# Two transformer layers and a three-branch block on one core: the change from one stage to the next by column halves and quarters

## The reference

```python
h = x                                                    # (1, 256, 1024)
u = rms_norm(h, g_mix[0]);  h = h + mla_stick_breaking_mixer(u, ...)     # first mixer
u = rms_norm(h, g_ffn[0]);  h = h + swiglu(u, w_gate[0], w_up[0], w_down[0])
u = rms_norm(h, g_mix[1]);  h = h + chunk_band_mixer(u, w_qkv, rel_bias, w_out)   # band mixer
u = rms_norm(h, g_ffn[1]);  h = h + swiglu(u, w_gate[1], w_up[1], w_down[1])
h = rms_norm(h, g_final)
hn = rms_norm(h, ln_g_2)                                 # second block
proj = hn @ w_in_2
branches = (moba_attention, dilated_attention, swa_sink_attention) on parts of proj
out = h + (sum of sigmoid(gates) * (branch @ w_branch)) @ w_out_2

def swiglu(u, w_gate, w_up, w_down):
    return (jax.nn.silu(u @ w_gate) * (u @ w_up)) @ w_down
```

## Time and profile before

| | |
|---|---|
| median of three runs | 1051.57 us |
| the profiled execution | 1051.47 us, of which its span is 1049.5 us |
| PE busy | 998.5 us (95% of the span) |
| DVE, ACT busy | 633.9 us (60%), 593.0 us (57%) |
| POOL busy | 21.3 us (2%), 10.64 us of it the mask's addition |
| all DMA traffic | 170.23 MB, mean 162 GB/s |

### The profile page before, as it was taken

The page is one execution under the profiler, slowest core; times in us unless marked ns, Lnnn a source line. Parts: engine busy times, 40 slices in busy tenths (PEclk is TensorE's granted clock), DMA queues, the critical chain, the costliest instruction groups (busy, mean ns, idle before and its releaser), DMA issues.

```text
span 1049.5 us, 13511 instructions
## 1 busy us (share of the span) xinstructions
PE 998.5 (95%) x5026; PEld 816.8 (78%) x5026; DVE 633.9 (60%) x780; ACT 593.0 (57%) x912; POOL 21.3 (2%) x21
## 2 busy tenths in 40 slices
PE   4999789999998999989999998999999998999998
PEld 3888668888887777768888887788787886778876
DVE  3576567555555574665555555668567566766654
ACT  4677464544454564554544454666756575856561
POOL 1000004000000000010000000000000000000000
PEclk9999999999999999999999999999999999999999
DMA  7435156655655433368555655454343333335550
GB/s 232 146 117 200 41 200 193 207 188 173 200 162 198 161 123 121 118 212 291 197 190 171 200 163 197 145 177 161 126 154 120 120 121 121 121 121 200 176 185 40
DMA packets 105691, 170.23 MB, mean 162 GB/s; under 512 B 3843, under 2 KB 65210, under 8 KB 105652
## 3 DMA queue, kind: packets, MB, share of 16 engines
q1 hardware_dynamic: 103040, 161.23, 46.6%
q0 software_dynamic: 2288, 8.37, 2.3%
q10 hardware_dynamic: 324, 0.10, 0.0%
HBM read 168.58 MB, written 1.11 MB: 162 GB/s over the span
## 4 chain that ended last, share of the span: by engine, by line
PE 89%; ACT 5%; DVE 4%; issue 1%; DMA 0%; ACTq 0%; DVEq 0%
PE acc L442 14%; PE acc L402 13%; PE acc L404 12%; PE acc L403 12%; PE pair_ps L404 7%; PE pair_ps L402 7%; PE pair_ps L403 7%; PE acc L612 4%; PE turn_ps L524 2%; PE pair_ps L512 1%; PE acc L492 1%; PE pair_ps L511 1%; ACT w_hi L922 1%; PE turn_ps L460 1%; ACT logit L1045 1%
## 5 line engine op out<-in xcount | busy, mean ns | idle before, releaser
L1538 DVE TENSOR_TENSOR w_lo<-w_raw,w_hi 128x2048 fp32r<-128x2048 f32 (+3 forms) x156 | 351.2, 2256 | 154.6 <-ACT w_hi L922 154.2
L922 ACT ACTIVATE w_hi<-w_raw 128x2048 fp32r<-128x2048 f32 (+3 forms) x156 | 290.3, 1863 | 86.8 <-PE acc L404 47.4
L402 PE MATMUL acc<-w_hi,uT_hi 128*128 128x512 f32 (+3 forms) x552 | 221.3, 401 | 9.9 <-DVE w_lo L1538 6.0
L404 PE MATMUL acc<-w_hi,uT_lo 128*128 128x512 f32 (+3 forms) x552 | 213.8, 387 | 0.0
L403 PE MATMUL acc<-w_lo,uT_hi 128*128 128x512 f32 (+3 forms) x552 | 213.2, 386 | 0.0
L402 PEld LDWEIGHTS acc<-w_hi,uT_hi 128*128 128x128 f32 x552 | 105.2, 191 | 35.1 <-issue 8.9
L402 PE MATMUL pair_ps<-w_hi,uT_hi 128*128 128x512 f32 x320 | 126.6, 396 | 0.0
L404 PE MATMUL pair_ps<-w_hi,uT_lo 128*128 128x512 f32 x320 | 125.0, 391 | 0.0
L403 PE MATMUL pair_ps<-w_lo,uT_hi 128*128 128x512 f32 x320 | 124.7, 390 | 0.0
L404 PEld LDWEIGHTS acc<-w_hi,uT_lo 128*128 128x128 f32 x552 | 104.8, 190 | 21.4
L403 PEld LDWEIGHTS acc<-w_lo,uT_hi 128*128 128x128 f32 x552 | 105.3, 191 | 18.1
(11 more groups left out here) (210 smaller groups left out, 1269.0 us busy)
## 6 DMA issues: line engine op xcount, KB each, us to landing
w_raw<-in_w_in SPq DMA_DIRECT2D x46, 1024.0 KB
w_raw<-in_w_gate SPq DMA_DIRECT2D x44, 512.0 KB
w_raw<-in_w_up SPq DMA_DIRECT2D x44, 512.0 KB
w_raw<-in_w_down SPq DMA_DIRECT2D x22, 1024.0 KB
w_raw<-in_w_out SPq DMA_DIRECT2D x12, 1024.0 KB
w_raw<-in_w_qkv SPq DMA_DIRECT2D x16, 512.0 KB
w_raw<-in_w_branch SPq DMA_DIRECT2D x6, 1024.0 KB
w_raw<-in_w_in SPq DMA_DIRECT2D x10, 512.0 KB
```

Source lines behind the costliest of these rows:

```text
L402: mm(o, xh, wh[:, k, :], start=first and k == 0, stop=False)
L404: done = mm(o, xl, wh[:, k, :], start=False, stop=last and k == len(kts) - 1)
L922: activation(w_hi[:, slot, 0:width], w_raw[:, slot, 0:width], ACT.Copy).then_inc(hi_done, 1)
L1538: v.tensor_tensor(w_lo[:, slot, 0:width], w_raw[:, slot, 0:width], w_hi[:, slot, 0:width].bitcast(f32), ALU.subtract).then_inc(lo_done, 1)
```

## The change

The closing unit of a stage is issued in four pieces of six matmuls: block 0 and 1 of the first column half, then block 0 and 1 of the second. Each piece has its own signal, and DVE adds each quarter of `h` by itself. PE puts the transposes of a finished quarter between the pieces; the last quarter's four are issued inside the next stage, ahead of the second token block of its first unit (`late`). The banks for the transposes are `pair_ps` for the first four tiles, and `turn_ps` or `acc[0]`, `acc[2]` for the others.

On DVE the split of the unit two ahead, which stood before the additions, stands between two halves of the `uT_lo` work. On ACT both squares move behind the first four `uT_hi`. At the second block the split of the third unit moves ahead of the second norm's squares on ACT, and on DVE ahead of its row factors. The input's transposes go by quarters too, and the result is stored in four pieces of 256 KB, not two of 512 KB.

POOL loads the band table in two halves at given units of swiglu 0 and fills the masked part with a constant (64 partitions x 1024 elements) in place of the addition. The four tables of the second block are loaded one by one, seven units apart, inside swiglu 1.

```diff
-        stream_banks = {norm: acc_banks + pair_banks if norm in (FFN0, FFN1) else turn_banks + pair_banks
+        stream_banks = {norm: pair_banks + ([acc[0][:, :], acc[2][:, :]] if norm in (FFN0, FFN1) else turn_banks)
...
-            for blk in range(TB):
-                sp.wait_ge(h_ready, 11 + blk)
-                sp.dma_start(out[0].rearrange("(b p) c -> p b c", p=P)[:, blk, :], h[:, blk, :]).then_inc(stored, 16)
+            for i, (blk, half) in enumerate(quarters):
+                c = slice(512 * half, 512 * half + 512)
+                sp.wait_ge(h_ready, 19 + i)
+                sp.dma_start(out[0].rearrange("(b p) c -> p b c", p=P)[:, blk, c], h[:, blk, c]).then_inc(stored, 16)
...
-            pool.dma_start(bias[:, 2:4, :, :], windows(rel_band, 256 - (P - 1), 513, 16)).then_inc(band_full, 16)
-            pool.tensor_tensor(band, band, m_chunk[:, :].unsqueeze(1).broadcast_to([P, 16, S]),
-                               ALU.add).then_inc(band_ready, 1)
+            for g in range(2):
+                pool.wait_ge(unit_used, FFN_UNITS[0] + 2 + 8 * g)
+                pool.dma_start(bias[:, 2 + g, :, :], windows(rel_band, 256 - (P - 1) + 8 * g * 513, 513, 8))\
+                    .then_inc(band_full, 16)
+            pool.memset(bias[0:64, 2:4, :, 0:64].rearrange("p a b c -> p (a b) c"), MASKED).then_inc(band_ready, 1)
...
             for g in range(4):
+                pool.wait_ge(unit_used, FFN_UNITS[1] + 2 + 7 * g)
...
+            def closing_unit(kt0, ahead=0, norm=None):
...
+                added = n.h
+                piece(0, 0).then_inc(proj_done, 1)
+                piece(1, 0).then_inc(proj_done, 1)
+                if norm is not None:
+                    pe.wait_ge(h_ready, added + 1)
+                    turn_part(norm, 0, 0)
+                piece(0, 1).then_inc(proj_done, 1)
+                if norm is not None:
+                    pe.wait_ge(h_ready, added + 2)
+                    turn_part(norm, 1, 0)
+                piece(1, 1).then_inc(unit_used, 1)
...
+                pe.wait_ge(h_ready, added + 3)
+                turn_part(norm, 0, 1)
+
+                def late():
+                    pe.wait_ge(h_ready, added + 4)
+                    turn_part(norm, 1, 1)
...
             def half_unit(o, x_hi, x_lo, kts, parts, blk, first, last):
+                if blk == 1 and n.late is not None:
+                    late, n.late = n.late, None
+                    late()
...
             def stream_norm(norm, gains=None):
+                split_banks(uT_hi, 0, 4, stream_banks[gains], gains)
                 for blk in range(TB):
-                    act.wait_ge(h_ready, n.h + blk + 1)
+                    act.wait_ge(h_ready, n.h + blk + 3)
                     row_squares(norm, h, D, blk)
-                    if blk == 0:
-                        split_banks(uT_hi, 0, KT, stream_banks[gains], gains)
+                split_banks(uT_hi, 4, 4, stream_banks[gains][2:], gains)
                 row_root(norm, D)
...
             stream_norm(FINAL, LN2)
+            slot_step()
...
+            def change_stream(norm):
+                for i in range(3):
+                    add_quarter(i)
+                banks = stream_banks[norm]
+                split_banks(uT_hi, uT_lo, 0, 2, banks, norm)
+                add_quarter(3, 1)
+                split_banks(uT_hi, uT_lo, 2, 2, banks[1:], norm)
+                slot_step()
+                split_banks(uT_hi, uT_lo, 4, 4, banks[2:], norm)
...
                 v.scalar_tensor_tensor(h[:, blk, :], h[:, blk, :], norms[:, FINAL, 2, blk:blk + 1],
                                        gain, ALU.mult, ALU.mult).then_inc(h_ready, 1)
+            slot_step()
             row_scales(LN2, D, times=FINAL)
-            project({1: head_sums, 3: head_sums}, after_unit={2: head_norm(0), 4: head_norm(1)})
+            project({1: head_sums, 3: head_sums}, after_unit={2: head_norm(0), 4: head_norm(1)}, early=1)
```

136 lines of the change are left out of this document (70 added, 66 removed).

## The result

Four executions of the changed kernel took 1042.63, 1043.12, 1043.65 and 1046.44 us: median 1043.38. Four of the kernel before, beside them, had a median of 1050.67. The ratio is 0.9917, 95% interval 0.9889 to 0.9945: faster by 7.3 us, 0.8%. The forecast was 1045.4, 2.0 us above the measured median. The profiled execution is the slowest of the four, 1046.44 with a span of 1044.5.

The account below looks back on a forecast made before the run. PE was taken as the bound, holding 89% of the chain. 1051.47 - 5.64 - 0.44 - 1.25 - 0.2 = 1043.9, plus 1.5 for the clock = 1045.4 us; 8-in-10 range 1042.6 to 1047.4.

Parts of the forecast that it names:

- Term 1: Changes into swiglu 0, band mixer and swiglu 1: quartered sums and interleaved transposes gain 1.89, 1.86 and 1.89, together 5.64 us.
- Term 3: TensorE's clock: a fall behind the new wait at the second block's third unit adds 1.5 us, between 0 and 2.4.
- Term 2: Second block: the norm chain ends the wait, so only 0.44 us of 1.9 arrives; PE waits 3.9 at the third unit.
- Term 5: The start: transposes by quarters let ACT's first work come earlier; gain 0.2 us, between 0 and 0.6.
- 0.3 of cover at the third unit: At the three changes, the third unit's `w_lo` is ready at 18.3 and PE wants it at 18.59.
- rivals C: Pieces gain less, held by quarters' additions or switches between transposes and matmuls: 1.1 each for 1.9, 1047.8 us; chance 0.13.
- D: Third unit's split comes late at the three changes, making the kernel slower: 1052.9 us if 2.8 late; chance 0.03.
- E: Every stage is bound by its factors like the second block, so the change does nothing it says: 1050.0 us; chance 0.05.
- Rival B: Second block gains like the others, 1.9 for 0.44, with no clock fall: 1042.5 us; chance 0.08.
- rival A: Clock doesn't fall behind the second block's new wait, or falls inside it: 1043.9 us; chance 0.25.
- Term 4: The end: last addition and last stored piece halve; gain 1.25 us, bounds 0.6 to 1.4.
- GpSimd: Mask's addition and table loads: the slowed split's 3.8 us were hidden and tables needed much later, so gain 0.

Follow-up runs that it names:

- e2_fill_wait: Changed kernel with 13 extra, never-read matmuls filling the wait ahead of the second block's third unit; median 1044.19 us, against 1043.4 for the changed kernel.
- c0_after_again: The changed kernel with no edit, timed and profiled once more; median 1043.4 us.
- f1_end_in_blocks: Changed kernel with its end as before: last unit, sums and output by row blocks, two transfers; median 1043.85 us.
- f3: Changed kernel with each change's last four transposes ahead of the next stage's first unit, not inside it; 1044.17 us.
- f5: Kernel before with GpSimd's part alone as changed (tables in pieces, fill for the addition); ratio to before 1.0003.
- g1: e3 with extra matmuls meant for three waits, the first nine standing where PE does not wait; 1040.88 us.
- e1: Changed kernel with the second block's third unit rounded and split where before did it, behind the second row factors; 1046.13 us.
- e3: Changed kernel with the last stage's second column group accumulated in acc2 and acc3, removing the third unit's wait; 1039.3 us, ratio to before 0.9878.
- f4_pool_back: Changed kernel with GpSimd's part as before (mask's addition, band tables in one transfer, four bias tables at once); 1050.64 us, against 1043.28 for the changed kernel.

## Why the prediction was right or wrong

**Direction: right. Mechanism: right for the changes of stage and the end, wrong for the clock's part in the median and for GpSimd's.** PE's order, the quarters' sums and the late transposes did what Term 1 said. Of the 2.0 us between forecast and median, 1.5 are Term 3; Terms 1 and 2 gave 0.5 and 0.3 more than forecast, and Term 5's 0.2 can't be seen.

**Term 1** (5.64): the three stretches gave 2.00, 2.10 and 2.07, together 6.17 (6.11 in the second profile, 0.47 more than forecast). The next stage began at 7.00 and not 7.12, without the wait of 0.2, and the second half unit's start (339.14 - 328.94 = 10.20) came 0.2 earlier than worked out. The 0.3 of cover at the third unit held: no wait there. With 2.0 us gained at each change and no wait at the third unit, rivals C, D and E fell.

**Term 2** (0.44): 22.94 to 22.16 is 0.78, with a wait of 3.48 for 3.9. The rounding, factor and copy steps came in the order forecast. ACT's rounding behind it started at 19.53 (660.52 - 640.99) and not at 19.9, and 0.2 of that was there when the product started (13.61 for 13.8). The wait itself, its releaser and DVE's `w_lo` between product and second factors are as forecast. Rival B fell.

**Term 3** (1.5): this is the step that failed, as a number to be added. The fall behind the new wait came in all three profiles of the changed kernel and cost 1.5 to 1.6, just as priced (201.32 and 201.43 for 199.80). But the forecast added it to an execution of before whose other falls it took as fixed. They are not: the clock fell in some profiles and not in others behind the waits at 417, 465, 864 and 877. Before had its own, one of them behind a change of stage that no longer has a wait. e2_fill_wait took away just the priced fall and the median stayed (1044.19 against 1043.4). The profile of before and the second one of the changed kernel show how the new fall can be paid for: behind the first closing unit, before pays one fall, at 881 (14.88 for 13.45), and c0_after_again one, at the new wait (201.43 for 199.80), with none at 876. Their spans differ by 8.1 (1049.5 and 1041.4). Without any clock term the stretches give 6.11 + 0.77 + 1.24 = 8.1 too, and 1051.47 - 8.1 = 1043.3, where the median lies. That is near rival A's 1043.9, though A's reason, no fall there, is not what happened. That the falls cancel *exactly* between the kernels isn't shown: two profiles of before and three of the changed kernel are too few to count them.

The Trainium skill, "TensorE: Matmul & The Clock Gate", "What's actually happening", adds that the watch on the array's activity is free-running and does not start over with the kernel. The three profiles of one program, the wait of 2.32 us with a fall in two and without one in the third, are in line with that, though no row here shows the watch itself. The forecast used only the half of the rule that says activity counts.

**Term 4** (1.25): 27.33 to 26.11, 1.22; f1_end_in_blocks gives 1.25.

**Term 5** (0.2): it can't be told. The first matmul came 0.59 earlier (18.43 for 19.02), but by the closing unit at 140 it was gone (140.37 for 140.32), and by profile that point varies between 137.75 and 141.19 in these kernels. Part of it is the fall at 123. From the wait at 109 to that unit it took 29.6 in the four profiles without this fall (f1, f3, f5, g1), 30.6 to 30.8 with it, and 32.0 in two where it lasted twice as long (e1, e3). The rest lies ahead of 109 and stays open.

**GpSimd** (0): no error in the sum, but the reason was wrong. The forecast had the rows: the slow split "ended at 171.15, 1.2 before PE used that unit and 0.5 before the `oT_lo` behind it was due". But Term 1 brings PE 2 us closer in that very stage. The cover was read from the schedule before and spent by other edits of the same change. With the part put back, f4_pool_back shows the bill: 2.5 us in each swiglu. In swiglu 0 the numbers close on the thinner cover: PE 2.0 nearer, the split's end 0.8 later behind the closing unit (171.50 - 139.84 = 31.66 for 171.15 - 140.32 = 30.83), less 0.5, is 2.3, and PE waited 2.33 for the `oT_lo`. In swiglu 1 the forecast had the later reload ("starts 7.4 later") and took no loss for it; with the tables asked for at once it stands behind them. A rival "GpSimd's part is what lets Term 1 arrive" should have stood there.

## What to carry to other kernels

Read the cover of each edit against the schedule that the other edits leave, not against the one of before: 0.5 us of slack was enough here until another edit took 2 us out of the same stage. Where a wait is filled or removed, look for the clock at the *next* waits as well, and price a fall as something that comes in some executions, by several profiles of both kernels. Where a stage is bound by a short chain between two units, give the next unit another accumulator: that was worth more (5.3 us in the trace, 2.9 and 4.1 in two comparisons of medians) than reordering the chain (1.4 in the trace).

## What the runs showed of the hardware

- Falls of the granted clock to the lower level (1.2 GHz) behind the same wait, with nearly the same busy time ahead of it (2.04 and 1.91 of 4 us), come in some executions and not in others. One costs 1.4 to 1.6 us here (14.88, 35.11 and 201.43 for 13.45, 33.62 and 199.80), and one that lasts twice as long 2.5 (15.94 for 13.45). The first 15 executions of before lay in three groups, 1049.5 to 1049.8, 1051.4 to 1051.9 and 1053.4 to 1053.9. That falls alone make the groups isn't shown: two profiles, 3.1 us apart, differ by 2.7 in falls, and later executions lie between the groups.
- DVE's split of weights, which reads two inputs from SBUF, all but stands still for as long as GpSimd's addition runs: it ended 2.15 us after the addition in one trace and 2.16 in another, at 8.65 and 6.11 us of length.
- It works the other way too: an addition that started inside such a split took 10.64 us, one that started behind it 9.06. DVE's operations that read PSUM kept their 0.69 and 0.87 us beside the addition, and a split beside the fill of 0.95 us kept its 2.29 (211.45 and 211.94 in the changed kernel).
